# A decoder trunk with three mixers: scores of the second and third branch as stacked matmuls of full height

## The reference

```python
qb_rot = rope(qb, positions)                       # second branch
k_sel, k_win = rope(ksb, positions), rope(kwb, positions)
s = einsum('bqhd,bkhd->bhqk', q, k) * scale        # scores of 'selected' and of 'window'
qc, kc = rope(qc, positions), rope(kc, positions)  # third branch, two maps a head
s = einsum('bqhmd,bkhmd->bhmqk', qi, k) * scale
t1 * cos - t2 * sin, t2 * cos + t1 * sin           # rope: halves of 32 of each 64 change places
```

## Time and profile before

| | |
|---|---|
| median of 3 runs | 1538.88 us (1538.76 to 1540.25) |
| the profiled execution | 1538.75 us, its span 1536.9 us |
| TensorE busy | 1496.8 us, 97% |
| VectorE, ScalarE, GpSimd busy | 61%, 41%, 5% |
| DMA engines, mean | 84 GB/s |
| granted clock | 0.997 |

### The profile page before, as it was taken

The page is one execution under the profiler, slowest core; times in us unless marked ns, Lnnn a source line. Parts: engine busy times, 40 slices in busy tenths (PEclk is TensorE's granted clock), DMA queues, the critical chain, the costliest instruction groups (busy, mean ns, idle before and its releaser), DMA issues.

```text
span 1536.9 us, 22588 instructions
## 1 busy us (share of the span) xinstructions
PE 1496.8 (97%) x7957; PEld 1205.0 (78%) x7957; DVE 941.2 (61%) x2197; ACT 636.7 (41%) x1499; POOL 75.4 (5%) x80
## 2 busy tenths in 40 slices
PE   8999999999999999999999999999999999999997
PEld 6777777887787777888787787787887777778885
DVE  6866765655657776554576667655556677854544
ACT  6533434433344444343444334334334444434343
POOL 1000000000000010000100000000000011000011
PEclk9999999999999999999999999999999999999998
DMA  7223332222223333332342324222222233233321
GB/s 197 84 83 90 97 76 62 56 70 62 69 63 96 90 83 83 98 108 72 106 108 69 103 76 115 64 52 66 63 62 76 70 96 89 70 101 99 89 86 72
DMA packets 250301, 129.50 MB, mean 84 GB/s; under 512 B 45690, under 2 KB 245972, under 8 KB 250196
## 3 DMA queue, kind: packets, MB, share of 16 engines
q1 hardware_dynamic: 250196, 128.13, 31.2%
HBM read 118.67 MB, written 2.10 MB: 79 GB/s over the span
## 4 chain that ended last, share of the span: by engine, by line
PE 87%; DVE 6%; ACT 3%; issue 2%; DMA 0%; POOL 0%; SPq 0%; ACTq 0%; POOLq 0%; DVEq 0%
PE D L732 24%; PE D L734 22%; PE D L733 22%; PE Ob L920 7%; PE S L879 5%; PE T L898 4%; DVE w_lo L1293 2%; ACT w_hi L1059 1%; PE Mb L936 1%; ACT probs L1173 1%; PE Mb L846 1%; PE Ob L924 1%; PE Mb L813 1%; DVE y_lo L1627 1%; DMA acc<-in_x_dram 0%
## 5 line engine op out<-in xcount | busy, mean ns | idle before, releaser
L732 PE MATMUL D<-h_hi,w_hi 128*128 128x512 f32 x1264 | 542.1, 429 | 9.9 <-DVE zs L1444 3.7
L734 PE MATMUL D<-h_lo,w_hi 128*128 128x512 f32 x1264 | 495.9, 392 | 0.0
L733 PE MATMUL D<-h_hi,w_lo 128*128 128x512 f32 x1264 | 494.3, 391 | 0.0
L1293 DVE TENSOR_TENSOR w_lo<-raw,w_hi 128x512 fp32r<-128x512 f32 (+2 forms) x504 | 295.0, 627 | 310.9 <-ACT w_hi L1059 310.7
L1059 ACT ACTIVATE w_hi<-raw 128x512 fp32r<-128x512 f32 (+2 forms) x504 | 264.6, 572 | 306.7 <-PE D L734 305.4
L732 PEld LDWEIGHTS D<-h_hi,w_hi 128*128 128x128 f32 x1264 | 238.5, 189 | 69.3 <-issue 18.4
L1173 ACT ACTIVATE probs<-probs,nmax 128x128 f32<-128x128 f32 (+3 forms) x256 | 141.9, 555 | 355.0 <-DVE nmax L1545 354.9
L734 PEld LDWEIGHTS D<-h_lo,w_hi 128*128 128x128 f32 x1264 | 237.4, 188 | 52.9
L733 PEld LDWEIGHTS D<-h_hi,w_lo 128*128 128x128 f32 x1264 | 239.4, 189 | 30.8 <-issue 0.5
L1545 DVE CUSTOM_DVE_ANT_0 probs<-S,maskb 128x128 f32<-128x128 f32 (+3 forms) x256 | 115.1, 487 | 48.4 <-PE S L879 29.8
L540 DVE COPY pT<-T 128x128 f32<-128x128 f32 (+3 forms) x160 | 77.4, 486 | 48.0 <-PE T L898 47.5
(11 more groups left out here) (243 smaller groups left out, 1498.9 us busy)
## 6 DMA issues: line engine op xcount, KB each, us to landing
raw<-in_w_in_dram SPq DMA_DIRECT2D x124, 512.0 KB, 3.9
raw<-in_w_in_dram SPq DMA_DIRECT2D x32, 256.0 KB, 3.7
raw<-in_w_out_dram SPq DMA_DIRECT2D x16, 512.0 KB, 4.1
raw<-in_w_ple_gate_dram SPq DMA_DIRECT2D x16, 512.0 KB, 4.2
rs<-rx SPq DMA_DIRECT2D x80, 64.0 KB, 2.0
raw<-in_cmp_w_k_dram SPq DMA_DIRECT2D x8, 512.0 KB, 3.8
raw<-in_cmp_w_v_dram SPq DMA_DIRECT2D x8, 512.0 KB, 3.8
raw<-in_w_br_a_dram SPq DMA_DIRECT2D x16, 256.0 KB, 2.9
```

The costliest lines, as they stand in the source:

```text
L732: pe.matmul(o, w_hi[:, sl, cs], hi[:, k, :], start=(k == 0), stop=False)
L733: pe.matmul(o, w_lo[:, sl, cs], hi[:, k, :], start=False, stop=False)
L734: ins = pe.matmul(o, w_hi[:, sl, cs], lo[:, k, :], start=False, stop=last)
L1293: TT(w_lo[:, sl, half], raw[:, ring(L, t, RAW), half], f(w_hi[:, sl, half]), ALU.subtract).then_inc(M["dve_lo"], 1)
```

## The change

The scores of the second and third branch become four matmuls of full height (128 rows). `q_st[b][h]` holds q_hi of head h in one half of the partitions and q_lo in the other; one k buffer holds k_hi twice, the next k_lo twice. So a head's score is q_st by k_hi and q_st by k_lo. The rotation writes hi and lo into `rx` and `rs` (now one tensor, `rxs`), and a new item "put" has SyncE place them with four DMAs a tile (64 rows by 512 for q, 64 by 1024 for k). The first branch stays. The evacuation of the next rotated tile into `rx`, and its swap, wait for the stores to have landed. "rot" comes 8 groups behind a tile's end and not 11, "put" 9 (kwb: 17, since its place is that of `flat`). In stage 3 kwb and vsb change places. `rb` is gone (`rs` takes its part), and `vbd` has its own memory, zeroed once at the start.

```diff
-    st[3] = [("qb", 0), ("w1v", 0), ("kwb", 0), ("w1v", 1), ("za", 3), ("w1v", 2), ("vsb", 0), ("w1v", 3), ("vwb", 0)]
+    st[3] = [("qb", 0), ("w1v", 0), ("vsb", 0), ("w1v", 1), ("kwb", 0), ("w1v", 2), ("za", 3), ("w1v", 3), ("vwb", 0)]
...
-                follow.append([8, ("swap", t)])
-                follow.append([11, ("rot", t)])
+                follow.append([6, ("swap", t)])
+                follow.append([8, ("rot", t)])
+                follow.append([17 if kind == "kwb" else 9, ("put", t)])
...
+        q_hi, q_lo = [part(0), part(2)], [part(1), part(3)]
+        k_hi, k_lo = [part(4), part(6)], [part(5), part(7)]
+        q_st = [[part(2 * b + h) for h in range(2)] for b in range(2)]
+        KC, KS, KW = (4, 8), 8, 12
...
+        def places(kind, n):
+            if kind[0] == "q":
+                return [(q_st[n % 2][h][half((h + part_) % 2), :], rxs[half(h), part_ * S:(part_ + 1) * S])
+                        for h in range(2) for part_ in range(2)]
+            at = {"ksb": KS, "kwb": KW, "kc": KC[n % 2]}[kind]
+            return [(part(at + 2 * h, 2)[half(g), :], rxs[half(h), :]) for h in range(2) for g in range(2)]
+
+        def place(M, eng, t):
+            kind, n, _ = tiles[t]
+            eng.wait_ge(M["qk_s"], rots.after(t))
             if kind == "kwb":
+                eng.wait_ge(M["pe_dense"], tile_of[("w1v", 3)] + 1)
+            elif kind != "ksb":
+                eng.wait_ge(M["pe_s"], rows_before[(4 if kind == "qb" else 8) + n - 1])
+            for dst, src in places(kind, n):
+                eng.dma_start(f(dst), src).then_inc(M["put_s"], 16)
...
                             if n > 1:
-                                sp.wait_ge(M["pool_rot"], n - 1)
+                                sp.wait_ge(M["put_s"], put_before[tiles[it[1]][:2]])
...
+                        if it[0] == "put":
+                            place(M, sp, it[1])
...
-                            if n > 1:
-                                pool.wait_ge(M["dve_rs"], n - 1)
-                            pool.tensor_tensor(rb[:], rs[:], sinT[:], ALU.mult).then_inc(M["pool_rot"], 1)
-                        if it[0] == "ht" and tiles[it[1]][0] == "w1v":
-                            pool.wait_ge(M["pe_dense"], it[1] + 1)
-                            pool.memset(vbd[:], 0.0).then_inc(M["vz_s"], 1)
+                            pool.tensor_tensor(rs[:], rs[:], sinT[:], ALU.mult).then_inc(M["pool_rot"], 1)
...
+                            else:
+                                at = {"c": KC[u % 2], "sel": KS, "win": KW}[m]
+                                for h in range(2):
+                                    pe.wait_ge(M["dve_max"], r - 1 + h)
+                                    qx = q_st[b][h][:, qs]
+                                    pe.matmul(Sc[h][:, 0:n], qx, part(at + 2 * h)[:, 0:n], start=True, stop=False)
+                                    pe.matmul(Sc[h][:, 0:n], qx, part(at + 2 * h + 1)[:, 0:n], start=False, stop=True).then_inc(M["pe_s"], 1)
...
                                 if r > 1:
-                                    act.wait_ge(M["sw_ld"], 64 * (r - 1))
                                     act.wait_ge(M["dve_rm"], r - 1)
+                                    act.wait_ge(M["put_s"], put_before[(kind, n)])
...
-                            if u is not None and u >= 2:
-                                act.wait_ge(M["pe_s"], rows_before[u - 1])
-                            A(hi_, rc[:], ACT.Copy).then_inc(M["act_rot"], 1)
+                            A(new_hi, rc[:], ACT.Copy).then_inc(M["act_rot"], 1)
```

More of the change, by code:

```diff
@@ L307, in hybrid_trunk @@
                 hids.add(kind)
-        elif it[0] == "rot":
-            qk_ready.add(tiles[it[1]][:2])
+        elif it[0] == "put":
+            placed.add(tiles[it[1]][:2])
         elif it[0] in ("vt", "gates", "ht", "kcmp", "vcmp", "cs", "ct", "Y"):
@@ L450, in hybrid_trunk @@
         hid = y_f[:, 2, :].rearrange("p (a g b c) -> p a g b c", a=2, g=2, b=4)
+        vbd = sb("vbd", [P, 2, P])
         kcmpT = sb("kcmpT", [P, 2 * C32])
@@ L556, in landed_at @@
             return slot_sum[t % RAW] + 16 * ((t - T0) // RAW + 1)
-        def rot_dst(kind, n):
-            if kind == "ksb":
-                return ks_hi, ks_lo, None
-            if kind == "kwb":
-                return kw_hi, kw_lo, None
-            u = (4 if kind == "qb" else 8) + n
-            return (k_hi[u % 2], k_lo[u % 2], u) if kind == "kc" else (q_hi[u % 2], q_lo[u % 2], u)
+        def places(kind, n):
[7 more added lines that the diff above has]
+            eng.wait_ge(M["qk_s"], rots.after(t))
+            if kind == "kwb":
+                eng.wait_ge(M["pe_dense"], tile_of[("w1v", 3)] + 1)
[3 more added lines that the diff above has]
+                eng.dma_start(f(dst), src).then_inc(M["put_s"], 16)
+        put_sum, at_ = {}, 0
+        for x_ in placed.order:
+            at_ += 16 * len(places(*x_))
+            put_sum[x_] = at_
+        put_before = {x_: put_sum[x_] - 16 * len(places(*x_)) for x_ in put_sum}
         with nc.Block() as block:
@@ L657, in _ @@
                 pool.memset(kcmpT[:], 0.0).then_inc(i_const, 1)
+                pool.memset(vbd[:], 0.0).then_inc(i_const, 1)
                 pool.memset(f(ck[:]), 0.0).then_inc(i_const, 1)
-                pool.wait_ge(i_const, 9)
+                pool.wait_ge(i_const, 10)
                 pool.affine_select(out=maskb[:, S - P:S], in_=maskb[:, S - P:S], compare_op=ALU.is_ge, fill=NEG, base=0,
@@ L865, in _ @@
                                 elif m == "c":
-                                    pe.wait_ge(M["qk_s"], qk_ready.after(("kc", u - 8)))
-                                elif m == "sel":
-                                    pe.wait_ge(M["qk_s"], qk_ready.after(("qb", u - 4)))
-                            if r >= 2:
-                                pe.wait_ge(M["dve_max"], r)
-                            ka, kb = {"a": (k_hi[b], k_lo[b]), "c": (k_hi[b], k_lo[b]),
-                                      "sel": (ks_hi, ks_lo), "win": (kw_hi, kw_lo)}[m]
+                                    pe.wait_ge(M["put_s"], max(put_sum[("qc", u - 8)], put_sum[("kc", u - 8)]))
+                                elif u > 4:
+                                    pe.wait_ge(M["put_s"], put_sum[("qb", u - 4)])
+                                else:
+                                    pe.wait_ge(M["put_s"], max(put_sum[("qb", 0)], put_sum[("ksb" if m == "sel" else "kwb", 0)]))
@@ L873, in _ @@
                             n = (i + 1) * P
                             qs = slice(i * P, n)
-                            for step, (qx, kx) in enumerate(((q_hi[b], ka), (q_lo[b], ka), (q_hi[b], kb))):
-                                last = step == 2 and m != "a"
-                                for h in range(2):
-                                    ps = slice(HD * h, HD * h + HD)
-                                    ins = pe.matmul(Sc[h][:, 0:n], qx[ps, qs], kx[ps, 0:n], start=(step == 0), stop=last)
-                                    if last:
-                                        ins.then_inc(M["pe_s"], 1)
@@ L882, in _ @@
-                            if m == "a":
-                                for h in range(2):
-                                    ps, hh = slice(HD * h, HD * h + HD), 2 * u + h
+                            if m == "a":
+                                if r >= 2:
+                                    pe.wait_ge(M["dve_max"], r)
+                                for step, (qx, kx) in enumerate(((q_hi, k_hi), (q_lo, k_hi), (q_hi, k_lo))):
+                                    for h in range(2):
+                                        pe.matmul(Sc[h][:, 0:n], qx[b][half(h), qs], kx[b][half(h), 0:n], start=(step == 0), stop=False)
+                                for h in range(2):
+                                    ps, hh = half(h), 2 * u + h
@@ L1529, in _ @@
                             t = it[1]
-                            hi_, lo_, u = rot_dst(*tiles[t][:2])
                             r = rots.after(t)
```

41 lines of the change are left out of this document (19 added, 22 removed).

## The result

The changed kernel took 1562.23 us (median of 4 runs, 1558.98 to 1565.13), the kernel before beside it 1539.57 us: a ratio of 1.0142 (95% interval 1.0129 to 1.0156), some 22 us slower. The forecast was 1531, with a range up to 1543. Its profiled execution took 1558.98 us, with a span of 1557.1, the fastest of the four. Executions of the kernel before spread from 1537.6 to 1545.3 us in all, at granted clocks from 0.997 to 0.992, so a difference of 2 us is near the edge of what the medians can tell.

A forecast was written before the change was run, and what follows sets the result against it. TensorE, busy 97% of the span, was taken to bound the kernel. Blocks -20.9, third branch +8.6, second branch +4.5 and stage 3 0 sum to -7.8 us, from 1538.75 to 1531 us; 8-in-10 range 1518 to 1543.

The forecast's parts named there:

- The blocks: Score blocks of second and third branch: four full-height matmuls cost 2.49 us per four widths, not 3.36; 20.9 us gained.
- less than 1 us in the third branch: TensorE's waits there for the other engines before the change, cited for the rival that the waits are hidden.
- The third branch's landing: Units 8 to 10: ScalarE's evacuation of kc waits for the stores of qc, delaying zs; +8.6 us, at most 18.
- each microsecond more goes through: Units 8 to 10, six places: each further microsecond ScalarE stands at kc reaches the gate tile; 1.8 us a place needed.
- The second branch: Rotation moved ahead of the end of the vc tile lengthens the chain to N; +4.5 us, from 0 to 12.
- Stage 3: New order (kwb after vsb): shorter wait for ScalarE, later zs of za; taken as 0, between -2 and +4 us.
- The stores of k at nothing: Stores of a k tile land in perhaps 6 us, first score comes 8 us or more later; cost nothing.
- Slower by the placing chain: Rival, chance 0.12: slow stores of qc hold ScalarE at kc in units 8 to 10, six times; 1545 us.
- The waits are hidden: Rival, chance 0.20: ScalarE's delays are made good before TensorE needs anything; losses 2 instead of 13, 1520 us.
- Nothing measurable: Rival, chance 0.14: losses near 18 to 23 us with the full gain; 1536 to 1541 us.
- the forecast's own 0.50: Chance given to the forecast of 1531 us itself, with its own range 1525 to 1536.
- The gaps stay: Rival, chance 0.04: the 0.18 us at a block's ends comes from something else; 3.6 gained, 13.1 lost, 1548 us.

The follow-up runs named there:

- stack: Kernel before with only the four full-height score matmuls in second and third branch, nothing placed (scores mix heads); 1524.05 us, ratio 0.9893.
- put8: Changed kernel with the stores of qc 8 groups behind the tile's end instead of 9, so ahead of the weight load; 1536.73 us, ratio 0.9966.
- rot11: Changed kernel with the rotation back at 11 groups and the stores at 12 (kwb's stay at 17); 1552.45 us, ratio 1.0078.
- cross_only: Changed kernel without two of the four stores of each qc tile (those of the hi part); 1544.77 us, ratio 1.0029.
- halfcols: Changed kernel with each store of a qc tile cut to 256 of its 512 columns, four issues kept; 1547.52 us, ratio 1.0041.
- b_rot8: Kernel before with GpSimd's product 6 and the rotation 8 groups behind a tile's end, not 8 and 11; no stores, no stacked scores; 1553.55 us, ratio 1.0080.
- b_st3: Kernel before with only stage 3 in the changed kernel's order (vsb before kwb); 1542.18 us, ratio 1.0011.
- best1: Changed kernel with own staging place for qc and kc of units 9 to 11, rotation at 11 everywhere, old stage 3 order; 1543.31 us, ratio 1.0020.
- best3: Changed kernel with staging place for units 9 to 11, rotation at 11 (stores 12) except qc and kc outside unit 9; 1525.96 us, ratio 0.9902.

## Why the prediction was wrong, point by point

**The blocks: right mechanism, but some 4 us of the gain never reach the end.** TensorE's rows are as forecast: 0.91, 0.72, 0.47 and 0.39 us for the four widths (forecast 0.91, 0.68, 0.46, 0.44), no gap ahead of a block. Taken block by block, from the dense matmul ahead to the second behind, the traces of `stack` and the kernel before differ by 20.0 us over all 96. By the ratio of `stack` 16.5 us reach the end of the kernel. Missed was that stage 11 gives its share back to a wait that is there anyway: "less than 1 us in the third branch" was read from a stretch that ends at 580 us, and TensorE's wait of 1.9 us for `y_q` stands at 599.88. Elsewhere a set is worth 0.75 and not 0.87; where those 0.12 go is open.

**The third branch's landing: the step that failed.** The mechanism was named, the place too, and its steps held up to one number. In stage 9, taken back by the 4.35 us that this stage started later: stores issued 502.7 (forecast 502.5), kc evacuated 508.6 (506.7), GpSimd done 514.5 (512.65), `zs` done 518.9 (516.7), gate tile 519.0 (516.8). The failed step is "For four stores of a q tile I take 4.2 us from first issue to landed". That is right for stores with nothing in front, as `put8` and `rot11` show with 4.3. The paragraph on the third branch had SyncE issue "one weight load (0.4) and then the stores", and charged the load with its issue time alone. Measured with it: 5.8. The load's own landing of 3.9 us stood on the page of the kernel before. `cross_only` and `halfcols` show that behind the load the bytes in flight count, and those two runs that the load just ahead is what made the landing long. The sum for the branch was +8.6 with a bound of 18; measured it is 24.7, that is +20.6 and the 4.1 us that `stack` gains there. Against `stack` the rest of the table is +7.4 in stage 3, +0.9 in stages 4 to 7 and +2.1 elsewhere.

**What each late microsecond costs.** Against `stack`, stages 8 and 9 lost 4.9 and 4.3 us (in the first layer; forecast 3.0 and 0.65, so 1.9 and 3.7 more) for a landing 1.4 and 1.9 us later than taken: in stage 9 more than one for one, against "each microsecond more goes through". Of the 3.7 there, 2.2 are the later start of the gate tile (519.0, forecast 516.8), the other 1.5 come behind it. Two things lay on top. VectorE's operation beside GpSimd's product took 1.62 us (the row at 517.62 above) where the same operation takes 0.62 at 476.31, with nothing beside it; the rotation started 0.34 us behind GpSimd's end. And TensorE's clock fell behind the longer stalls: some 40 dense matmuls of this profile are 0.43 us apart and not 0.23, 8 us in all; in the profile of the kernel before there is no such stretch between the start and the end.

**The second branch: right in place, too large by some 2 us.** Forecast +4.5 by the rotation's place. V waits for `tmp` six times, 3.5 us, and `rot11`, with the move undone, has the full gain in stages 4 to 6. `b_rot8` shows +4.1, on the kernel before. But against `stack` the changed kernel loses only 0.9 in stages 4 to 7, or 2.6 if `stack`'s slow stretch of 1.7 us is taken out: stages 4, 5 and 7 cost some 0.5 each as forecast, and stage 6, which was counted in, costs nothing.

**Stage 3: wrong by 7 us.** I took 0, between -2 and +4. The first wait, for ScalarE, did not shrink from 1.35 to 0.4: TensorE now waits 1.36 us for the evacuation into `y_f` at that place. The wait for `rx` itself did go, to 0.15. And kwb's rotation ahead of za's end costs more than the 1 us taken for it: the wait for `zs` there is 3.4 us in the first layer and 2.9 in the second, where it was 1.3 before and 1.95 with the new order alone (`b_st3`), and slow matmuls stand behind it.

**The stores of k at nothing: right, with a wrong landing.** Behind a load those of kc took 8.1 to 9.9 us from first issue to landed in the changed kernel, and not "perhaps 6"; the room was large enough. In no run with kc where the change has it did a first score wait for them by more than 0.5 us.

**The rivals.** "Slower by the placing chain" is what happened, at 0.12. It had the right waits and the right number of places, and needed 1.8 us a place more; but it hung them on the issue time of a store (1.2 us each), which came out at 0.62 as forecast. It named "a queue with weight loads in it" as a point for it and gave that no price. "The waits are hidden", "Nothing measurable" and the forecast's own 0.50 rested on the 4.2. "The gaps stay" is ruled out by the rows: no gap ahead of a block, and four matmuls in 0.91.

## What to carry to other kernels

A DMA that someone waits for is priced with what was issued ahead of it, not from a row of the same kind that flew alone: look at what stands before it on its queue, and how long that takes to land. Where a short store and a large prefetch come together, issue the store first; the prefetch has slots of slack and the store has none. Before moving an operation by one fixed distance for all tiles, price each place: here the same rotation wants 11 groups in the second branch and 8 for the qc and kc of stage 7 (with 11 there, `best1` loses 2.5 and 1.0 us in that stage where `best3` gains 0.9 and 0.7), and the best kernel uses both.

## What the runs showed of the hardware

- SBUF to SBUF stores of 64 rows from one queue: four of 128 KB had landed 4.2 to 4.3 us after the first issue where the last load had gone out 3.4 us or more before (`rot11` and `put8`, stages 8 and 9), and 5.8 us where 512 KB had gone out 0.47 us before (the changed kernel). The pages' medians for 128 KB are 2.4 us in `put8` and 3.9 in the changed kernel; for 256 KB 3.9 in `rot11` and 5.3 in the changed kernel; 64 KB (32 rows) took 2.0. Behind the load, each further 256 KB in flight cost about 1 us. GpSimd as second issuer (0.5 us an issue) didn't change that.
- Six half-height matmuls of 512 columns took 0.90 us and 0.18 more at their two ends; four of full height took 0.91, with nothing ahead of them.
- TensorE's granted clock fell to the 1.2 GHz level in stretches of 3 to 10 dense matmuls. In the changed kernel each such stretch after the first 30 us stands behind a stall of 1.9 us or more, but not each stall has one: the same wait of 1.9 us for `y_q` (599.88 in the kernel before) was followed by 6 to 8 slow matmuls in the first layer of the changed kernel and of `b_rot8`, and by none in the kernel before. A stall of 2 us can so cost 3.4. In `stack` a stretch (at 960.3) came behind a wait of only 0.77 us, so the runs give no length below which a wait is safe.
- A VectorE operation with two operands in SBUF that starts while a GpSimd product of 128x512 runs took about 1 us longer: 1.62 at 517.62, where it takes 0.62, and 1.64 for `y_lo` at 473.91, where it takes 0.69 (rows below, changed kernel). In the kernel before the order was the other way once: VectorE's operation began at 511.33, 0.07 us ahead of GpSimd's, and took its 0.62, and the product took 1.70 instead of 1.28. The Trainium skill, GPSIMD Engine Reference (Specifications), lists the SBUF interfaces of the two engines as shared where VectorE reads two inputs there; these rows agree.

```profile
473.73 1.26 POOL L704 TENSOR_TENSOR rxs<-rxs,sinT 128x512 f32<-128x512 f32 x1 [14.29 <-DMA rxs<-rxs]
...
473.91 1.64 DVE L1642 TENSOR_TENSOR y_lo<-y_f,y_hi 128x512 fp32r<-128x512 f32 x1 [1.65 <-ACT y_hi L1211]
...
476.31 0.62 DVE L1574 SCALAR_TENSOR_TENSOR probs<-probs,coef 128x384 f32<-128x384 f32 x1
```

The same two operations in the kernel before, with VectorE's first:

```profile
511.33 0.62 DVE L1559 SCALAR_TENSOR_TENSOR probs<-probs,coef 128x384 f32<-128x384 f32 x1
...
511.40 1.70 POOL L684 TENSOR_TENSOR rb<-rs,sinT 128x512 f32<-128x512 f32 x1 [6.75 <-DMA rs<-rx]
```
